# Rotary embedding of the two hybrid layers: from GpSimd to VectorE

## What is computed

```
def rms_norm(x, g):
    xf = x.astype(jnp.float32)
    y = xf * lax.rsqrt(jnp.mean(xf * xf, axis=-1, keepdims=True) + EPS)
    return (y * g.astype(jnp.float32)).astype(x.dtype)
...
def apply_rope(x, cos, sin):
    x1, x2 = jnp.split(x, 2, axis=-1)
    return jnp.concatenate([x1 * cos - x2 * sin, x2 * cos + x1 * sin], axis=-1)
...
    mq = apply_rope(rms_norm(split_heads(m_q.astype(f32), MOBA_HEADS), moba_qn_g), cos, sin)
    mk = apply_rope(rms_norm(split_heads(m_k.astype(f32), MOBA_HEADS), moba_kn_g), cos, sin)
```

## Time and profile before

| | |
|---|---|
| median of 3 runs | 1666.17 us (1664.1 to 1668.17) |
| the profiled execution | 1668.48 us, its span 1666.7 us |
| busy share of the span: TensorE, its weight loads | 93%, 75% |
| VectorE, ScalarE, GpSimd | 71%, 53%, 8% |
| the chain that ended last: TensorE, "issue", VectorE, ScalarE | 51%, 29%, 14%, 5% |
| rotary work, layer 0 and layer 1 | about 47 to 126 us and 552 to 630 us |

### The profile page before, as it was taken

How to read it: one execution, slowest core, us unless ns; L and a number is a source line. 1 busy time by engine, 2 the same in 40 slices (tenths; PEclk the granted TensorE clock), 3 DMA queues, 4 the chain that set the end, 5 groups by cost and what they waited for, 6 DMA issues and landing times.

```text
span 1666.7 us, 19902 instructions
## 1 busy us (share of the span) xinstructions
PE 1552.5 (93%) x7224; PEld 1253.3 (75%) x7224; DVE 1177.2 (71%) x1517; ACT 879.1 (53%) x1137; POOL 135.0 (8%) x133
## 2 busy tenths in 40 slices
PE   7999999999998999999999997887886999999995
PEld 6787778888876887777878776676775888777774
DVE  5787777677676787677776676554466455889985
ACT  5644765544444644665544443354434444777872
POOL 0470000000000461000000000000000000000000
PEclk9999999999999999999999997997997999999998
DMA  7534434576764544334577666241205455899991
GB/s 293 177 131 158 141 127 150 204 268 251 279 255 166 174 149 152 127 128 150 175 275 290 260 235 242 101 135 68 90 13 196 152 178 186 287 353 354 347 360 48
DMA packets 45440, 326.06 MB, mean 196 GB/s; under 512 B 5280, under 2 KB 5280, under 8 KB 6688
## 3 DMA queue, kind: packets, MB, share of 16 engines
q1 hardware_dynamic: 38304, 278.94, 46.7%
q0 software_dynamic: 4608, 33.56, 5.2%
q10 hardware_dynamic: 2432, 12.30, 1.9%
HBM read 323.73 MB, written 1.05 MB: 195 GB/s over the span
## 4 chain that ended last, share of the span: by engine, by line
PE 51%; issue 29%; DVE 14%; ACT 5%; DMA 0%; ACTq 0%; DVEq 0%; POOL 0%; POOLq 0%
PE PS L147 49%; DVE PR L179 4%; PE PS L152 3%; DVE w_lo L168 3%; ACT w_hi L161 2%; DVE PR L168 2%; ACT S L161 1%; DVE h_lo L168 1%; DVE G L168 1%; ACT L161 1%; DVE at_lo L168 1%; DVE S L179 0%; DVE S L168 0%; DMA cact<-c 0%; DVE a_lo L179 0%
## 5 line engine op out<-in xcount | busy, mean ns | idle before, releaser
L168 DVE TENSOR_TENSOR w_lo<-stage,w_hi 128x1024 fp32r<-128x1024 f32 x532 | 659.2, 1249 | 343.8 <-ACT w_hi L161 338.3
L161 ACT ACTIVATE w_hi<-stage 128x1024 fp32r<-128x1024 f32 x532 | 560.0, 1058 | 543.2 <-PE PS L147 539.6
L147 PE MATMUL PS<-w_hi,a_hi 128*128 128x512 f32 x1088 | 442.0, 406 | 12.0 <-DVE w_lo L168 6.6
L147 PE MATMUL PS<-w_lo,a_hi 128*128 128x512 f32 x1088 | 428.7, 394 | 0.0
L147 PE MATMUL PS<-w_hi,a_lo 128*128 128x512 f32 x1088 | 428.2, 394 | 0.0
L147 PEld LDWEIGHTS PS<-w_hi,a_hi 128*128 128x128 f32 x1088 | 207.4, 191 | 63.6 <-issue 10.9
L147 PEld LDWEIGHTS PS<-w_hi,a_lo 128*128 128x128 f32 x1088 | 206.9, 190 | 45.1
L147 PEld LDWEIGHTS PS<-w_lo,a_hi 128*128 128x128 f32 x1088 | 207.5, 191 | 41.4 <-issue 1.2
L147 PE MATMUL PS<-w_hi,h_hi 128*128 128x512 f32 (+1 forms) x352 | 140.3, 399 | 3.7 <-DVE PR L168 1.6
L147 PE MATMUL PS<-w_lo,h_hi 128*128 128x512 f32 (+1 forms) x352 | 137.5, 390 | 0.0
L147 PE MATMUL PS<-w_hi,h_lo 128*128 128x512 f32 (+1 forms) x352 | 137.2, 390 | 0.0
(11 more groups left out here) (239 smaller groups left out, 1693.3 us busy)
## 6 DMA issues: line engine op xcount, KB each, us to landing
stage<-wall SPq DMA_DIRECT2D x170, 1024.0 KB, 4.9
stage<-wexp SPq DMA_DIRECT2D x96, 1024.0 KB, 5.0
PR<-wada POOLq DMA_DIRECT2D x32, 1024.0 KB, 8.3
G<-gate_b ACTq DMA_DIRECT2D x2, 1536.0 KB, 8.5
PR<-rows ACTq DMA_DIRECT2D x1, 2048.0 KB, 12.1
lsm<-small ACTq DMA_DIRECT2D x3, 563.0 KB, 3.6
X<-x_in ACTq DMA_DIRECT2D x1, 1024.0 KB, 5.0
PR<-rows ACTq DMA_DIRECT2D x1, 1024.0 KB, 7.8
```

What stands on the lines that cost most here:

```text
L147: ins = self.e.matmul(out, lhsT, rhs, start=start, stop=stop, skip_group_check=True)
L161: self.tell(self.e.activation(out, in_, func, **kw), sem, chain)
L168: self.tell(self.e.tensor_tensor(out, a, b, op), sem, chain)
```

## The change

VectorE now does everything in the rotary lane but the power: the square ahead of its reduction, and after GpSimd's power the two multiplies and the rotation. GpSimd is left with one small operation (128 x 8) per group. The signal `rope_sq` falls away, `rope_scaled` is now told by the power, and `rope_done` by VectorE. The steps of the generators are at the same places of `ORDER` as before.

```
         def rope_pool(g, l):
...
             for i in range(4):
...
                 g.wait_ge("rope_var", 4 * l + i + 1)
-                scale = st[:, 232:240]
-                g.tt(scale, scale, mhalf[:, 0:8], ALU.pow)
-                g.tt(v, v, scale.unsqueeze(2).broadcast_to([P, H8, HD]), ALU.mult, sem="rope_scaled")
-                yield
...
+                g.tt(st[:, 232:240], st[:, 232:240], mhalf[:, 0:8], ALU.pow, sem="rope_scaled")
+                yield
+                yield
+
+        def rope_dve(v, l):
+            for i in range(4):
+                x = chunk(4 + i // 2)[:, i % 2, :]
+                h, gain, t = heads(x, H8), lay("qn" if i < 2 else "kn"), i % 2
+                evac_done(v, l, 4 + i // 2)
+                v.tt(rope_sq, x, x, ALU.mult)
+                v.reduce(st[:, 224:232], heads(rope_sq, H8), ALU.add)
+                v.ts(st[:, 232:240], st[:, 224:232], 1.0 / HD, EPS, ALU.mult, ALU.add, sem="rope_var")
+                yield
+                v.wait_ge("rope_scaled", 4 * l + i + 1)
+                v.tt(h, h, st[:, 232:240].unsqueeze(2).broadcast_to([P, H8, HD]), ALU.mult)
+                v.tt(h, h, gain.unsqueeze(1).broadcast_to([P, H8, HD]), ALU.mult)
...
                 for s in range(2):
-                    g.tt(A[:, :, s, :], x[:, :, s, :], cos, ALU.mult)
-                    g.tt(B[:, :, s, :], x[:, :, 1 - s, :], sin, ALU.mult)
-                g.tt(x[:, :, 0, :], A[:, :, 0, :], B[:, :, 0, :], ALU.subtract)
-                g.tt(x[:, :, 1, :], A[:, :, 1, :], B[:, :, 1, :], ALU.add, sem="rope_done")
-                yield
-
-        def rope_dve(v, l):
-            for i in range(4):
-                v.wait_ge("rope_sq", 4 * l + i + 1)
-                v.wait_ge("rope_scaled", 4 * l + i)
-                v.reduce(st[:, 224:232], heads(rope_sq, H8), ALU.add)
-                v.ts(st[:, 232:240], st[:, 224:232], 1.0 / HD, EPS, ALU.mult, ALU.add, sem="rope_var")
-                yield
+                    v.tt(A[:, :, s, :], x[:, :, s, :], cos, ALU.mult)
+                    v.tt(B[:, :, s, :], x[:, :, 1 - s, :], sin, ALU.mult)
+                v.tt(x[:, :, 0, :], A[:, :, 0, :], B[:, :, 0, :], ALU.subtract)
+                v.tt(x[:, :, 1, :], A[:, :, 1, :], B[:, :, 1, :], ALU.add, sem="rope_done")
                 yield
```

More of the change, by code:

```diff
@@ L97 @@
 gla_kv gla_state gla_out gla_copied gla_var gla_rs gla_silu gla_y
-rope_sq rope_var rope_scaled rope_done
+rope_var rope_scaled rope_done
 moba_turned moba_qk
@@ L949, in rope_pool @@
         def rope_pool(g, l):
[L950 to L955, removed]
             for i in range(4):
-                v, gain = heads(rows(i), H8), lay("qn" if i < 2 else "kn")
-                if i == 0:
-                    square(0)
                 g.wait_ge("rope_var", 4 * l + i + 1)
-                scale = st[:, 232:240]
-                g.tt(scale, scale, mhalf[:, 0:8], ALU.pow)
-                g.tt(v, v, scale.unsqueeze(2).broadcast_to([P, H8, HD]), ALU.mult, sem="rope_scaled")
+                g.tt(st[:, 232:240], st[:, 232:240], mhalf[:, 0:8], ALU.pow, sem="rope_scaled")
                 yield
[L966 to L974, removed]
-                    g.tt(A[:, :, s, :], x[:, :, s, :], cos, ALU.mult)
-                    g.tt(B[:, :, s, :], x[:, :, 1 - s, :], sin, ALU.mult)
-                g.tt(x[:, :, 0, :], A[:, :, 0, :], B[:, :, 0, :], ALU.subtract)
-                g.tt(x[:, :, 1, :], A[:, :, 1, :], B[:, :, 1, :], ALU.add, sem="rope_done")
                 yield
@@ L987, in rope_dve @@
                 yield
+                v.wait_ge("rope_scaled", 4 * l + i + 1)
+                v.tt(h, h, st[:, 232:240].unsqueeze(2).broadcast_to([P, H8, HD]), ALU.mult)
+                v.tt(h, h, gain.unsqueeze(1).broadcast_to([P, H8, HD]), ALU.mult)
+                x = x.rearrange("p (h s d) -> p h s d", h=H8, s=2)
+                A, B = (a.rearrange("p (h s d) -> p h s d", h=H8, s=2) for a in (rope_a, rope_b))
+                cos, sin = (const(n)[:, t * 32:(t + 1) * 32].unsqueeze(1).broadcast_to([P, H8, 32]) for n in ("cos", "sin"))
+                for s in range(2):
+                    v.tt(A[:, :, s, :], x[:, :, s, :], cos, ALU.mult)
+                    v.tt(B[:, :, s, :], x[:, :, 1 - s, :], sin, ALU.mult)
+                v.tt(x[:, :, 0, :], A[:, :, 0, :], B[:, :, 0, :], ALU.subtract)
+                v.tt(x[:, :, 1, :], A[:, :, 1, :], B[:, :, 1, :], ALU.add, sem="rope_done")
                 yield
```

## The result

| | before | after |
|---|---|---|
| median of 4 runs each, same chip | 1665.13 us (1664.07 to 1668.17) | 1680.70 us (1676.89 to 1682.95) |
| span of the profiled execution | 1666.7 us | 1675.1 us |
| mean of one w_lo, whole span | 1249 ns | 1222 ns |

The ratio is 1.0088, with a 95% interval of 1.0064 to 1.0112: slower by about 15 us, where 13.9 were forecast. The profiled execution of after is the shortest of its four runs, so its trace shows less than the medians do. One execution of the kernel before (2371.5 us, mean granted clock 0.605) and one of experiment 3 (1782.32 us, 0.831) fell into a slow state and are left out of every median and ratio here.

What follows compares the result with a forecast made beforehand. VectorE's lateness, holding ScalarE's w_hi copies and TensorE's weights, was taken as the bound. Per layer 4.5 + 2.15 = 6.65 us, two layers 13.3, plus 0.6 for the clock: 13.9, so 1680.0 us, range 1672 to 1690.

Steps and rivals of the forecast that it cites:

- What bounds the kernel: From 83 us VectorE never catches up; ScalarE's w_hi copies queue behind its gate sum; TensorE's weight halves have no slack.
- The tail, 4.15 us: VectorE's two multiplies and six rotation operations per group, priced by its own rows at 0.69 and 0.42 us.
- Rival 1: Tails cost 5.6 us, since they read short strided pieces and rewrite their source: 1689 us, chance 8%.
- rival 3: Added VectorE operations as cheap as the lower bound, or some 3 us of TensorE slack: 1674 us, chance 14%.
- Relief of 7.3 us: Between 83 and 117 us, w_lo, qk steps and qk multiplies on VectorE shorten by this, undisturbed by GpSimd.
- one wait of 2.1: VectorE, undisturbed, overtakes ScalarE once near 87 us and waits 2.1 us for a w_hi.
- The gate sum 4.5 us late: VectorE's gate sum ends at 120.8 instead of 116.3, delaying ScalarE and TensorE's half at 121.30.
- Nothing is handed on before 83 us: VectorE's added 5.6 us before 83 us is caught up by the w_lo at 83.14, so no shift there.
- The fourth tail, net 2.15, total 6.65 per layer: Ahead of the gate chain: 4.15 us added less 2.0 relief; with the gate sum's 4.5, the loss per layer.
- The clock, 0.6 us in layer 0: After TensorE's longer gaps the lower clock costs layer 0 what layer 1 already showed, 0.6 us.
- rival 2: TensorE's clock falls after the longer gaps in both layers and stays down: 1685 us, chance 8%.
- rival 5: Faster: with GpSimd silent, `ml_abs` comes earlier and TensorE's 1.9 us waits vanish in both layers: 1662 us, chance 4%.

Runs made afterwards that it cites:

- experiment 3: The changed kernel with the four products of the fourth group's rotation computed twice, 1.8 us more on VectorE per layer: 1682.0 us against 1666.58, ratio 1.0104.
- Experiments 1: The changed kernel with the fourth group's tail behind the mlstm gate chain instead of ahead of it, both layers: 1670.31 us against 1666.58, ratio 1.0028.
- experiment 10: The kernel before with only the first group's square per layer moved to VectorE: 1662.86 us against 1665.45, one execution, too few for a verdict.
- experiment 5: The changed kernel itself, measured and profiled once more: 1679.34 us against 1666.3 for the kernel before, ratio 1.0091.
- experiment 8: The kernel before, rotary work still on GpSimd, with both key groups five steps later, behind the gate chain: 1659.16 us against 1666.3, ratio 0.9958.

## Why the prediction was right

**What bounds the kernel: right.** The places named (gate sum, ScalarE's queue, the half at 121, the half at 129) are where the time was lost. Experiments 1 and 3 show that a microsecond of VectorE's work ahead of the gate chain is about a microsecond of the kernel's time, once per layer: 4.18 us moved gave back 3.6 and 4.3, 1.83 added cost 1.6 to 2.7, clock included.

**The tail, 4.15 us: right**, 4.18. Strided runs, two tensors read and a source rewritten cost nothing beside the plain rows. Rival 1 falls, and so does rival 3, for which two tensors read would have had to cost no more than one.

**Relief of 7.3 us and one wait of 2.1: right.** The wait came as 0.62 and 1.44 us, 2.06 together.

**The gate sum 4.5 us late: right**, measured against VectorE's own start of the stretch: 3.57 by the clock on the wall (119.90 against 116.33) plus the 0.97 of lead at its head, 4.54. ScalarE's wait grew by 13.26 - 8.71 = 4.55.

**"Nothing is handed on before 83 us": wrong**, by 0.97 us in the kernel's favour, of which 0.84 are the change's doing (experiment 10). That step counted the disturbance of the w_lo only and left out gla's operation at 48.71, whose relief experiment 10 shows.

**The fourth tail, net 2.15, total 6.65 per layer: right, less the lead.** TensorE's half at 128.93 starts at 134.77, 5.84 us later, with the 0.97 it is 6.8. Of the two gaps, "about 3" came as 2.82, and "about 4.7" as 4.65, the loss to the clock between them counted in (experiment 5). As plain waits they are 1.23 to 2.82 and 2.11 to 3.04, because TensorE had used the rest at the lower clock. The shift of about 6 us held up to 491 us; layer 1 lost 6.11 more.

**The clock, 0.6 us in layer 0: right in one execution of two.** Behind the last wait of the stretch TensorE kept full speed in the first execution and lost 0.5 us in experiment 5. Inside the gaps the lower clock cost nothing, since VectorE's lateness covered it, which the prediction had held against rival 2. That rival had the lower clock right (behind one gap of layer 0 in the first execution, two in the second, and two or three of layer 1) and the loss wrong. Elsewhere the clock moved parts of single executions by 1 to 3 us in either direction.

**The sum: right in its parts, and its closeness in part luck.** The medians show 13.0 and 15.6 us, where 13.9 were said. The stretches themselves cost 12.0 and 12.5. The 0.5 and 3.6 us between are not assigned to a place: they go with the mean granted clock of the runs, which is an association and no cause that was shown. That 1680.70 lies 0.7 us from 1680.0 owes something to this: the lead made the layers cheaper than said, and the unassigned rest made up for it.

**The marks to look for.** w_lo 1.219 us as said; GpSimd's busy time 48.4 us instead of 45, the 3.4 us being powers that took longer (below). The answer to the wrong sign (rival 5) is experiment 8: silence of GpSimd ahead of the gate chain, with two small reductions of VectorE moved behind it, is worth some 7 us, so the mechanism of that rival exists. It was paid for with two pairs of tail and square that cost more than they freed.

## What to carry to other kernels

Before work is moved between engines, find the operation that another engine's in-order queue waits for, and count what lies ahead of it in the receiving queue, at the price of that queue's own rows; shares of busy time (71% here) say nothing about it. A neighbour that slows the critical engine can be better moved in time than in place: half of the same GpSimd work, put behind the gate chain with the two reductions that belong to it, gained 7 us, where taking all of it over cost 13 to 16. And how far it can be put off is set by its reader, where a wait that nothing covers may also cost the clock.

## What the runs showed of the hardware

The power that stays did not slow VectorE, but was slowed itself. GpSimd in after, layer 0 (start us, us):

```profile
57.85 2.55 POOL L205 TENSOR_TENSOR st<-st,mhalf 128x8 f32<-128x8 f32 x1 [37.78 <-DVE st L175]
70.18 2.54 POOL L205 TENSOR_TENSOR st<-st,mhalf 128x8 f32<-128x8 f32 x1 [9.79 <-DVE st L175]
102.42 1.64 POOL L205 TENSOR_TENSOR st<-st,mhalf 128x8 f32<-128x8 f32 x1 [29.70 <-DVE st L175]
```

The two long ones began 0.17 us into a w_lo (57.68 and 70.01 us, each 1.22 us long as ever); the third ran beside qk steps. In the kernel before, the power at 58.09 us began ahead of the w_lo at 58.37 and took 1.64. So an operation of VectorE already under way held the power up by 0.9 us, and a power already under way did not hold VectorE up (1.23 us for the w_lo at 58.37). With larger operations both were longer: GpSimd's squares took 1.90 us instead of 1.04, w_lo 1.66 instead of 1.22. The Trainium skill (SBUF — State Buffer, SBUF: two separate sides) says that a VectorE operation with two SBUF inputs and a GpSimd operation that reads SBUF exclude each other for a whole instruction, whichever starts first. By that rule, the trace agrees where w_lo came first, and not where the power came first. What is shown against the rule is this one small power: GpSimd's square of 47.80 us, begun ahead of gla's operation of 48.71, did make that operation longer (2.06 us instead of 1.22).

The same wait did not always have the same clock behind it. Behind 1.91 us at the half of 128.93 the kernel before kept full speed, and the kernel of experiment 10 fell to the lower level; behind 1.94 us in layer 1 the kernel before fell too. A wait of 1.33 us was followed by the lower level in layer 1 of after (from 624.65 us) and not at 114.76 in layer 0.
